# First modulation of a two-layer trunk: its products on TensorE in four column groups instead of on VectorE

## The reference

```python
cond = jax.nn.silu(c)                                   # c: (1, 2048)
for layer in range(2):
    shift, scale, gate = jnp.split((cond @ w_ada[layer] + b_ada[layer])[:, None, :], 3, axis=-1)
    h = rms_norm(x, norm_g[layer]) * (1.0 + scale) + shift
    (qkv_a, z_a, ..., glu_in, ..., gate_raw) = split_columns(h @ w_in[layer])
    ...                                                 # gated delta rule, convolution, sparse attention
    x = x + gate * (merged @ w_out[layer])
```

## Time and profile before

| | us |
|---|---|
| median of 3 runs | 2197.31 (2196.27 to 2199.36) |
| the profiled execution, by the same clock as those runs | 2198.33 |
| its span in the trace, first to last instruction | 2196.5 |
| PE busy in the span | 2137.2 (97%) |
| DVE, ACT, POOL busy | 1215.8, 960.8, 1662.2 |

### The profile page before, as it was taken

How to read it: one execution, slowest core, us unless ns; L and a number is a source line. 1 busy time by engine, 2 the same in 40 slices (tenths; PEclk the granted TensorE clock), 3 DMA queues, 4 the chain that set the end, 5 groups by cost and what they waited for, 6 DMA issues and landing times.

```text
span 2196.5 us, 37664 instructions
## 1 busy us (share of the span) xinstructions
PE 2137.2 (97%) x14782; PEld 1945.9 (89%) x14782; DVE 1215.8 (55%) x2147; ACT 960.8 (44%) x1056; POOL 1662.2 (76%) x676
## 2 busy tenths in 40 slices
PE   5799999999999999999989999999999999999999
PEld 3799999987889988788989999999788998888899
DVE  6959974847555455545562884756656445431110
ACT  3344444484333534444344443446633354444442
POOL 1568768767765899998859885877667579988876
PEclk8899999999999999999999999999999999999999
DMA  9976535444543699898965564544445358956654
GB/s 375 399 254 231 183 119 184 161 145 163 176 158 115 228 341 342 301 352 323 353 221 189 195 215 136 164 163 155 161 157 170 126 187 320 345 198 203 219 194 153
DMA packets 123391, 481.71 MB, mean 219 GB/s; under 512 B 13492, under 2 KB 17876, under 8 KB 110580
## 3 DMA queue, kind: packets, MB, share of 16 engines
q1 hardware_dynamic: 123092, 479.65, 61.7%
q10 hardware_dynamic: 160, 0.13, 0.0%
HBM read 473.29 MB, written 6.31 MB: 218 GB/s over the span
## 4 chain that ended last, share of the span: by engine, by line
PE 46%; POOL 28%; issue 20%; DVE 3%; ACT 1%; DVEq 1%; POOLq 0%; ACTq 0%
POOL wl L554 28%; PE ps L955 14%; PE ps L956 14%; PE ps L957 14%; DVE score L1646 1%; PE ps L1316 0%; ACT wh L575 0%; POOLq L553 0%; PE ps L1323 0%; PE ps L1304 0%; PE ps L1250 0%; ACTq L752 0%; PE ps L1115 0%; PE ps L1239 0%; PE ps L1272 0%
## 5 line engine op out<-in xcount | busy, mean ns | idle before, releaser
L554 POOL TENSOR_TENSOR wl<-raw,wh 128x1024 fp32r<-128x1024 f32 x672 | 1661.9, 2485 | 521.3 <-ACT wh L575 519.5
L575 ACT CAST wh<-raw 128x1024 fp32r<-128x1024 f32 x672 | 703.9, 1050 | 1103.9 <-PE ps L957 919.3
L955 PE MATMUL ps<-ah,wh 128*128 128x256 f32 x3008 | 868.9, 289 | 20.7 <-DVE al L1516 14.7
L956 PE MATMUL ps<-al,wh 128*128 128x256 f32 x3008 | 857.6, 285 | 0.0
L957 PE MATMUL ps<-ah,wl 128*128 128x256 f32 x3008 | 857.2, 285 | 0.0
L955 PEld LDWEIGHTS ps<-ah,wh 128*128 128x128 f32 x3008 | 584.3, 194 | 27.2 <-DVE al L1516 15.0
L956 PEld LDWEIGHTS ps<-al,wh 128*128 128x128 f32 x3008 | 584.2, 194 | 4.2 <-issue 3.9
L957 PEld LDWEIGHTS ps<-ah,wl 128*128 128x128 f32 x3008 | 583.9, 194 | 0.0
L955 PE MATMUL ps<-wh,ah 128*128 128x512 f32 (+1 forms) x832 | 319.7, 384 | 0.9 <-POOL wl L554 0.9
L957 PE MATMUL ps<-wh,al 128*128 128x512 f32 (+1 forms) x832 | 317.1, 381 | 0.0
L956 PE MATMUL ps<-wl,ah 128*128 128x512 f32 (+1 forms) x832 | 317.1, 381 | 0.0
(11 more groups left out here) (280 smaller groups left out, 1680.7 us busy)
## 6 DMA issues: line engine op xcount, KB each, us to landing
raw<-w_piece SPq DMA_DIRECT2D x672, 512.0 KB, 3.3
modw<-w_ada SPq DMA_DIRECT2D x64, 1024.0 KB, 7.3
adaw<-w_first SPq DMA_DIRECT2D x32, 1024.0 KB, 8.5
gbias<-b_gate SPq DMA_DIRECT2D x24, 256.0 KB, 3.8
xs<-xt SPq DMA_DIRECT2D x2, 2048.0 KB, 13.0
skew<-stage SPq DMA_DIRECT2D x8, 256.0 KB, 5.3
bias<-skew SPq DMA_DIRECT2D x2, 1024.0 KB, 8.2
gcb<-grow SPq DMA_DIRECT2D x8, 256.0 KB, 3.6
```

Source lines behind the costliest of these rows:

```text
L554: nc.gpsimd.tensor_tensor(wl[:, s], raw[:, s], wh[:, s].bitcast(F32), ALU.subtract).then_inc(sem("w_split"), 1)
L575: A.copy(wh[:, s], raw[:, s]).then_inc(sem("w_rounded"), 1)
L955: M.matmul(o, lh, rh, start=start, stop=False, skip_group_check=True)
L956: M.matmul(o, lh, rr, start=False, stop=False, skip_group_check=True)
```

## The change

1. The products of the first modulation go to PE. `cond` is spread to 32 equal columns (`cond32`, 128x32 per channel tile). `ada_piece(n)` makes eight matmuls of 256 columns per block: for each of two row tiles, four of 32 output partitions, one column group each. PSUM bank 7 then holds four groups of 32 equal rows.
2. `ada_rows(q)` (DVE) copies that bank, 128x256, to `adarow`; `ada_turn(q)` (PE) brings the totals to the partitions with two matmuls against every 32nd column of the identity, four columns each. `ada_part` and `ada_sum` are gone.
3. The blocks of quarter q+1 stand among the products of quarter q on PE: one each behind the first, second and third piece, five behind the fourth; the turn stands in the middle of the fifth piece.
4. x goes to SP's queue ahead of the blocks, the parameters behind block 5, and the pieces of `w_in` stand in other places among the blocks. All four quarters of x are scaled at once.
5. Bias rows four heads at once: the table lies on 128 partitions (`rbt` 128x2, `hotsb` four times, 256 KB instead of 64), so that four matmuls of 32 rows each, one row group each, make four heads. ACT takes four banks out with one copy, or two.

```diff
@@ SP's queue
-            sp.dma_start(hotsb[0:BUCKETS, :], hot).then_inc(sem("hot_landed"), 16)
-            sp.dma_start(rbt[0:BUCKETS, :], rel_bias).then_inc(sem("rb_landed"), 16)
+            sp.dma_start(rbt[:], rel_bias).then_inc(sem("rb_landed"), 16)
+            sp.dma_start(hotsb[:], hot).then_inc(sem("hot_landed"), 16)
+            sp.dma_start(xs[:], xt.rearrange("p (k t) -> p k t", t=T)).then_inc(sem("x_landed"), 16)
...
-                if n == 2:
-                    sp.dma_start(xs[:], xt.rearrange("p (k t) -> p k t", t=T)).then_inc(sem("x_landed"), 16)
+                if n == 5:
                     sp.dma_start(par[:], params).then_inc(sem("par_landed"), 16)
...
+        PIECES_BEHIND = {7: (0, 1), 8: (2,), 9: (3,), 10: (4,), 11: (5,)}
...
-                        for i, at in ((5, 10), (4, 9), (3, 7), (2, 6), (1, 4), (0, 2)):
-                            if n >= at and (n - at) % 8 == 0 and n - at < 24:
-                                chunk(6 * ((n - at) // 8) + i)
-                    for i in range(18, 24):
+                        for at in (n % 8, n % 8 + 8):
+                            for i in PIECES_BEHIND.get(at, ()):
+                                if n >= at:
+                                    chunk(6 * ((n - at) // 8) + i)
+                    for i in range(20, 24):
                         chunk(i)
@@ ACT
-            for h in range(HEADS):
-                act.wait_ge(sem("bias_mm"), h + 1)
-                if h + 4 < HEADS:
-                    bias_row(h + 4)
-                A.copy(stage[h // 6][:, h % 6, :], ps[:, h % 4, :]).then_inc(sem("bias_row"), 1)
+            bias_rows(0)
...
+            bias_rows(1)
             root_mean(0)
@@ PE
+            def ada_piece(n):
+                q, j = n // 8, n % 8
+                pe.wait_ge(ada_landed[j % 4], 16 * (n // 4 + 1))
+                for m in range(2):
+                    kt = 2 * j + m
+                    for c in range(4):
+                        mm = M.matmul(ps[32 * c:32 * c + 32, 7, 0:T], cond32[:, kt],
+                                      adaw[j % 4][:, m, c // 2, (c % 2) * T:(c % 2 + 1) * T],
+                                      start=kt == 0, stop=kt == KT - 1)
+                mm.then_inc(sem("ada_used"), 1)
...
+            def ada_turn(q):
+                pe.wait_ge(sem("ada_rows"), q + 1)
+                for c in range(2):
+                    mm = M.matmul(pb[2][:, 8 * q + 4 * c:8 * q + 4 * c + 4], adarow[:, c * P:(c + 1) * P],
+                                  ident[:, 0:P:32], start=True, stop=True)
+                mm.then_inc(sem("ada_turned"), 1)
...
                     for q in range(4):
-                        ada_sum(q)
-                        for pair in range(3):
-                            part_gemm(hc, pair, H, 4 * q, 4, G_IN, paired=pair == 0)
-                            hc += 2
+                        ahead = {0: (0,), 1: (1,), 2: (2,), 3: (3, 4, 5, 6, 7)} if q < 3 else {}
+                        for i in range(4):
+                            first_piece(q, i)
+                            for n in ahead.get(i, ()):
+                                ada_piece(8 * (q + 1) + n)
+                        first_piece(q, 4, 0, 1)
+                        if q < 3:
+                            ada_turn(q + 1)
+                        first_piece(q, 4, 1, 2)
+                        first_piece(q, 5)
+                        hc += 6
@@ DVE
+            V.tensor_copy(cond32[:], spread(cond[:], 2, [P, KT, 32])).then_inc(sem("cond_ready"), 1)
...
-                            ada_part(0, 0, 10)
                             normed_x()
-                        normed_quarter(q)
-                        ada_part(q, ADA_SIDE + 1 if q else 10, KT)
-                        if q == 0:
+                            for n in range(4):
+                                normed_quarter(n)
                             dve.wait_ge(sem("par_landed"), 16)
                             dve.wait_ge(sem("con_landed"), 16)
-                        if q < 3:
-                            ada_part(q + 1, 0, ADA_SIDE)
+                        ada_rows(q)
```

More of the change, by code:

```diff
@@ L196, in trunk @@
         ssum = tiny("ssum", [HEADS])
-        rbt = tiny("rbt", [HEADS])
+        rbt = tiny("rbt", [HEADS // 4])
         epsb = tiny("epsb", [3])
@@ L270, in trunk @@
         acc = sb("acc", 170, [2, D])
+        cond32 = sb("cond32", 170, [KT, 32])
+        adarow = sb("adarow", 172, [T])
         rst = sb("rst", 146, [T])
@@ L587, in _, with bias_rows @@
             act.wait_ge(sem("con_landed"), 16)
-            def bias_row(h):
-                A.activation(rbb[0:BUCKETS, h % 4], ones[0:BUCKETS, :], ACT.Copy, scale=rbt[0:BUCKETS, h:h + 1]
-                             ).then_inc(sem("rbb_ready"), 1)
-            for h in range(4):
-                bias_row(h)
-            for h in range(HEADS):
-                act.wait_ge(sem("bias_mm"), h + 1)
-                if h + 4 < HEADS:
-                    bias_row(h + 4)
-                A.copy(stage[h // 6][:, h % 6, :], ps[:, h % 4, :]).then_inc(sem("bias_row"), 1)
+            for r in range(2):
+                A.activation(rbb[:, r], ones, ACT.Copy, scale=rbt[:, r:r + 1]).then_inc(sem("rbb_ready"), 1)
+            def bias_rows(r):
+                act.wait_ge(sem("bias_mm"), r + 1)
+                if r == 0:
+                    A.copy(stage[0][:, 0:4, :], ps[:, 0:4, :]).then_inc(sem("bias_row"), 1)
+                else:
+                    A.copy(stage[0][:, 4:6, :], ps[:, 0:2, :])
+                    A.copy(stage[1][:], ps[:, 2:4, :]).then_inc(sem("bias_row"), 1)
+            bias_rows(0)
             act.wait_ge(sem("x_landed"), 16)
@@ L627, in _ @@
                 if layer == 0:
-                    for q in range(3):
-                        rounds(hc, RING, hc % RING)
+                    for q in range(4):
+                        rounds(hc, 2, hc % RING)
                         h_high(q)
-                        rounds(hc + RING, 2, (hc + RING) % RING)
+                        rounds(hc + 2, 4, (hc + 2) % RING)
                         hc += 6
-                    rounds(hc, 1, hc % RING)
-                    h_high(3)
-                    rounds(hc + 1, 5, (hc + 1) % RING)
-                    hc += 6
                     act.wait_ge(sem("w_used"), hc)
@@ L1027, in sum_tiles @@
                 M.matmul(pb[1][:, 0:T], ones, sqs[:], start=True, stop=False)
-            pe.wait_ge(sem("hot_landed"), 16)
-            for h in range(HEADS):
-                pe.wait_ge(sem("rbb_ready"), h + 1)
-                if h >= 4:
-                    pe.wait_ge(sem("bias_row"), h - 3)
-                M.matmul(ps[:, h % 4, :], rbb[0:BUCKETS, h % 4], hotsb[0:BUCKETS, :], start=True, stop=True
-                         ).then_inc(sem("bias_mm"), 1)
-            for q in range(4):
-                sum_squares(0, q)
@@ L1039, in ada_sum, with bias_rows @@
-            def ada_sum(q):
-                pe.wait_ge(sem("ada_summed"), q + 1)
-                for part in (SHIFT, SCALE):
-                    for j in range(4 * q, 4 * q + 4):
-                        mm = M.matmul(pb[2][:, part * KT + j:part * KT + j + 1], acc[:, part, j * P:(j + 1) * P],
-                                      ones[:, 0:1], start=True, stop=True)
-                mm.then_inc(sem("ada_turned"), 1)
+            def bias_rows(r):
+                pe.wait_ge(sem("rbb_ready"), r + 1)
+                if r:
+                    pe.wait_ge(sem("bias_row"), r)
+                for j in range(4):
+                    g = slice(32 * j, 32 * j + 32)
+                    mm = M.matmul(ps[:, j, :], rbb[g, r], hotsb[g, :], start=True, stop=True)
+                mm.then_inc(sem("bias_mm"), 1)
@@ L1048, in mod_sum @@
+            sum_squares(0, 0)
+            sum_squares(0, 1)
+            ada_piece(1)
+            sum_squares(0, 2)
+            sum_squares(0, 3)
+            for n in range(2, 8):
+                ada_piece(n)
+            ada_turn(0)
             def mod_sum(part, n):
@@ L1496, in quarter_mods @@
                     at = n * KT + 4 * q
-                    last = V.tensor_tensor(mods[:, at:at + 4], pb[2][:, at:at + 4], p_(0, "b_ada", at, 4), ALU.add)
+                    turned = pb[2][:, 8 * q:8 * q + 8].rearrange("p (c n h) -> p n h c", n=2, h=2)[:, n]
+                    last = V.tensor_tensor(mods[:, at:at + 4].rearrange("p (h c) -> p h c", c=2), turned,
+                                           p_(0, "b_ada", at, 4).rearrange("p (h c) -> p h c", c=2), ALU.add)
                 if q == 3:
```

44 lines of the change are left out of this document (16 added, 28 removed).

## The result

The change makes the kernel slower. In five runs beside five of the kernel before it takes 2208.78 us (median; 2204.8 to 2212.26) against 2197.42 (2196.27 to 2199.36): a ratio of 1.0048, 95% interval [1.0037, 1.006]. Forecast were 2186.3. The profiled execution is the slowest of the five (2212.26 us); its span is 2210.4, so 13.9 us more than the span of 2196.5 before, where the medians differ by 11.4.

A forecast was written before the change was run, and what follows sets the result against it. The DMA engines were taken to set the first stage's pace, 27.4 us a quarter. The last quarter starts at 121.6, plus 17.1 and 1.2 ends at 139.9 against 151.3; 11 off 2197.31 gives 2186.3 us, range 2183.0 to 2192.5.

The forecast's parts named there:

- DVE's copy and the steps from totals to h: Behind each quarter's last block: 3.2 us and about 1 more, beside PE's products, done 1 us ahead of PE.
- The ring of four blocks allows it: Block buffers in the first stage: block 28 can be issued once block 24 is used, about 3 us ahead of need.
- The cadence of 27.4 us: First stage: the DMA engines already set the distance between quarters, 27.4 us, so the change can't shorten it.
- the clock: Rival, chance 0.13: TensorE's clock falls in each quarter's waits, or bias row groups don't run together; gain 4.4 to 8 us.
- c of 1.5 or more: Rival: c us per block on PE, which becomes the bound; 2203 or 2257 us, chances 0.07 and 0.05.
- a DMA share under 0.95 with blocks issued late: Sign of being wrong in the first stage: the ring of block buffers, not the DMA engines, sets the pace.
- The products on PE: First modulation: four column groups at once, 0.88 us a block, 0.39 for switching; PE needs 26.1 us a quarter.
- The first products near 38 us: First quarter: the first products of h come near 38 us instead of 49.51; only lead, the DMA engines set the rest.
- Edits at nothing: Start of the first stage: bias rows end near 11 us, ahead of block 0; scaling x and the small copies cost nothing.
- The last quarter's clock: First stage's last quarter: the clock's fall costs 2.4 us before; half, 1.2, was counted after the change.
- All later stages move as they are: Behind the first stage nothing else changes, so its 11.4 us carry over to the whole span.
- Piece 24: Behind the last quarter: ready at 137.7 us, wanted by PE at 139 to 140, so covered by 1 to 2 us.

The follow-up runs named there:

- e4: The changed kernel with five block buffers instead of four and each quarter's first two pieces behind its sixth block; 2186.15 us, ratio 0.9958 to the kernel before.
- e1: The changed kernel, but POOL subtracts only 64 of 1024 columns of each of the first 24 pieces (output not the reference's); 2192.9 us, ratio 0.9985.
- the second alone: The changed kernel with five buffers for the blocks instead of four; 2196.31 us, ratio 1.0002 to the kernel before.
- g4: The changed kernel with POOL subtracting only 64 of 1024 columns of the first 24 pieces, and five block buffers; 2184.02 us, ratio 0.994.
- h3: The kernel before with only the bias rows made four heads at once, x left behind block 2; 2195.33 us, ratio 0.9989.
- g3: The kernel before, products left on VectorE, with x first, parameters behind block 5 and bias rows four heads at once; 2193.29 us, ratio 0.9977.
- h4: The kernel before with only x first in the queue and the parameters behind block 5, bias rows as they were; 2196.18 us, ratio 0.9996.
- g1: e4 with x back behind block 2, as in the kernel before; 2192.51 us, ratio 0.9976 to the kernel before.
- g2: e4 with the bias rows one head at a time in one row group, as before; 2191.97 us, ratio 0.9982 to the kernel before.

## Why the prediction was wrong, step by step

- **"DVE's copy and the steps from totals to h take 49.51 - 46.30 = 3.2 us ... and are done 1 us ahead of PE"**: this step failed first. The 3.2 us were right for an idle POOL (e4: 38.69 to 41.68, 3.0 us). The change put POOL's split beside them, and PE got its h 7.5 to 8.1 us behind the totals. In the fourth quarter four subtractions ran beside them, and the last step ended after 10.7. The edit that did it, the new places of the pieces, was costed by its bytes alone. What else the pieces bring, a POOL instruction of 2.4 us each, had no line in the sum.
- **"The ring of four blocks allows it: block 28 ... about 3 us ahead of need"**: failed second. The margin held only for the forecast's own starts, the first near 38.5 us and one every 27.4. With the first products at 44.9 the queue had run out before block 12 could be issued (0.05 at 50 to 52 us), and the lateness comes back in each quarter. A margin of 3 us was none beside a term, the way to h, that I had no bound for. Mending the first step alone takes 13.4 us off the fourth quarter's start (e1), the second alone 14.1 (e2), both 24.8 (g4).
- **The cadence of 27.4 us** as a floor: near it, 28.0 in e4 and 28.1 in g4. It is none for the distance of the starts to the last tenth: h3 has 26.8, behind a first quarter as late as before. As a forecast: wrong, 34.4, because "no engine is full" was not among the cases. My rivals had PE as the bound, or the clock; none had a loop of waits, and the mechanism on the slower side that I priced (c of 1.5 or more) was not the one that came. The last of the signs of being wrong, a DMA share under 0.95 with blocks issued late, did name it, and it came (0.89), but without a price or a chance.
- **The products on PE**: right, and a little better than taken. Block and piece follow each other every 4.06 us (54.69 to 58.75), of which 24 products of 0.119 are 2.86: a block with the switches into and out of it takes 1.2 us, forecast 0.88 + 0.39. The block is 0.86 of it and switching about 0.33, so PE's need is 17.1 + 8 x 0.86 + 5 x 0.33 = 25.6 us, forecast 26.1. The four column groups are 4.0 times as fast as one (3.45 to 0.86). The Trainium skill's 3.07 times ("TensorE: Matmul & The Clock Gate", Part 3, Measured speedup vs the span model; it stands there for four row tiles of 512 columns), which I had set aside, would have been low here.
- **The first products near 38 us**: 44.9. Of the 6.9, 4.6 are the lock, and most of the rest is block 7, which landed 1.5 us later than in my sum and was made at half clock.
- **Edits at nothing**: the bias rows and x first were put down as cover only, with no gain of their own. In the kernel before they bring 4.4 us by themselves (g3). The wait of VectorE for the root was in the trace of before and I had not used it.
- **The last quarter's clock**: I took half of 2.4 us for gained. In e4, with PE busy to the last, all of it was (PEclk 1.00 from 125.7 on); in the changed kernel PE stood still for 3.9 us ahead of the last quarter (144.31 to 148.21) and started at the lower level, PEclk 0.50 from 149 to 153.
- **"All later stages move as they are"**: not quite. The last quarter starts 16.5 us later than before, the span is 13.9 longer. Two later falls of the clock (at 1157 and 1355 us) lasted 3.4 us each in place of 6.8, so 3.4 us are lost over both in place of 6.8. That is 3.4 less, and 16.5 - 3.4 = 13.1; the 0.8 to 13.9 are not accounted for.
- **Piece 24**: as forecast; in e4, where it comes at the forecast's time, PE waits for nothing from 126 to 175 us.

What stays open: why the clock's later falls come in some kernels and not in others (no run isolates them), and how much of e4's 10.5 us would be left where they came back.

## What to carry to other kernels

When an edit moves a transfer, move everything that hangs on it in your sum, to the engine that works on it when it lands, and look for the same pair of engines side by side somewhere in the trace: one instruction with two lengths (0.75 and 2.86 us) is a warning that its length depends on company. Where a buffer is freed by an engine that itself waits for what that buffer feeds, write the loop down, once around, and compare it with the fullest engine's time; the larger of the two is the cadence. And undo the edits that "cost nothing" one by one and together, since here two of them, worth 2.3 us and nothing clear of noise singly (h3, h4), brought 4.4 together, as much as the change's main part.

## What the runs showed of the hardware that I had not expected

- Each of VectorE's instructions between SBUF and SBUF that starts beside a GpSimd subtraction stops until that one is done: 0.16 becomes 0.82 to 1.51 us, 0.41 becomes 2.3 to 2.4, 0.68 becomes 2.7 to 2.9, 0.75 becomes 2.86. With the running sum from PSUM the length stays (1.28). It is counted as busy time of VectorE, not as a wait. GpSimd's own subtraction is held too when VectorE has begun first (3.3 in place of 2.35 us at 33.20 in the kernel before).
- Four column groups of 32 with fp32 operands of 256 columns run 4.0 times as fast as one (0.86 to 3.45 us for 16 instructions), and going in and out costs about 0.33 us together.
- One core's 16 DMA engines hold 408 to 419 GB/s from HBM over 84 us (e4), the other cores idle.
- A fall of the TensorE clock far from the change (at 277 us) is missing from e4, whose later stages are the same code, and its 3.4 us are a quarter of the difference between the two spans. It is missing from h4 as well, and not from g1 and g2, so it is no mark of the change.
